# Seven block products in the pooled groups' output projection, and a chunk mask as eight score rows

## The reference, cut to what matters

```python
k_chunk = jnp.arange(s) // CHUNK                       # CHUNK = 64
sc = jnp.einsum('bqhd,bkhd->bhqk', qb, k) * scale
sc = jnp.where(k_chunk[None, :] <= q_chunk[:, None], sc, -jnp.inf)
```

```python
u, z = jnp.split(h @ w_in, 2, axis=-1)
p = causal_multiscale_pool(u).reshape(B, S, N_POOL_GROUPS, GROUP_WIDTH)
y = jnp.einsum('bsgc,gcd->bsgd', p, w_group).reshape(B, S, A_WIDTH_2) * scale
return (y * jax.nn.silu(z)) @ w_out                    # x = x + gate * this
```

## Time and profile before

| | |
|---|---|
| median of three runs | 2355.61 us (2354.32 to 2355.93) |
| span of the profiled execution | 2354.7 us, 0.9 us under that median |
| TensorE busy | 2328.3 us, 99% of the span, 11617 matmuls |
| TensorE weight loads | 1943.6 us (83%) |
| VectorE, GpSimd, ScalarE busy | 1535.8 us (65%), 1254.7 us (53%), 860.4 us (37%) |
| mean granted TensorE clock | 0.999 of full speed |

### The profile page before, as it was taken

One profiled execution on the slowest core, in us unless ns is written; L12 is line 12 of the kernel. 1 busy time (PEld: TensorE's weight loads), 2 busy tenths in 40 slices (PEclk: granted clock), 3 DMA queues, 4 the chain that ended last, 5 costly groups with the idle time before them and its releaser, 6 DMA issues.

```text
span 2354.7 us, 32347 instructions
## 1 busy us (share of the span) xinstructions
PE 2328.3 (99%) x11617; PEld 1943.6 (83%) x11617; DVE 1535.8 (65%) x1839; ACT 860.4 (37%) x1596; POOL 1254.7 (53%) x724
## 2 busy tenths in 40 slices
PE   9999999999999999999999999999999999999998
PEld 7888789888888888888888888778878788889887
DVE  7825556524578678788777777874572967147885
ACT  5212555612543222222222443122231244157773
POOL 4533955144145666766777434573654733467743
PEclk9999999999999999999999999999999999999999
DMA  5511011031011333333331111112121122210033
GB/s 220 157 45 46 19 19 37 1 116 45 19 42 50 117 124 117 125 125 117 123 124 64 63 45 45 58 53 78 54 76 67 58 67 109 79 37 24 24 115 137
DMA packets 67340, 178.85 MB, mean 76 GB/s; under 512 B 6994, under 2 KB 13908, under 8 KB 65120
## 3 DMA queue, kind: packets, MB, share of 16 engines
q1 hardware_dynamic: 57760, 147.80, 19.0%
q10 hardware_dynamic: 9104, 27.51, 3.4%
q0 software_dynamic: 368, 2.10, 0.5%
HBM read 161.61 MB, written 15.77 MB: 75 GB/s over the span
## 4 chain that ended last, share of the span: by engine, by line
PE 76%; DVE 6%; issue 4%; POOL 2%; ACT 1%; DMA 0%; POOLq 0%; DVEq 0%; ACTq 0%; SPq 0%
PE ps L704 21%; PE ps L705 20%; PE ps L707 20%; PE ps L854 4%; PE ps L832 3%; PE ps L842 2%; DVE trail L3532 1%; POOL split_lo L1653 1%; PE ps L2404 1%; PE ps L2420 1%; PE ps L2419 1%; PE ps L2389 1%; PE ps L2390 1%; ACT p L955 1%; PE ps L508 0%
## 5 line engine op out<-in xcount | busy, mean ns | idle before, releaser
L704 PE MATMUL ps<-h_hi,split_hi 128*128 128x512 f32 x1546 | 606.4, 392 | 3.7 <-DVE h_lo L3214 1.3
L705 PE MATMUL ps<-h_lo,split_hi 128*128 128x512 f32 x1546 | 601.1, 389 | 0.0
L707 PE MATMUL ps<-h_hi,split_lo 128*128 128x512 f32 x1546 | 536.2, 389 | 0.0
L1511 POOL TENSOR_TENSOR split_hi<-raw,cf 128x1024 fp32r<-128x1024 f32 x64 | 125.4, 1959 | 427.8 <-PE ps L707 373.4
L704 PEld LDWEIGHTS ps<-h_hi,split_hi 128*128 128x128 f32 x1546 | 290.7, 188 | 64.5 <-issue 2.5
L707 PEld LDWEIGHTS ps<-h_hi,split_lo 128*128 128x128 f32 x1546 | 290.8, 188 | 61.3
L705 PEld LDWEIGHTS ps<-h_lo,split_hi 128*128 128x128 f32 x1546 | 290.8, 188 | 56.4 <-issue 0.2
L1600 POOL TENSOR_TENSOR split_lo<-raw,split_hi 128x512 fp32r<-128x512 f32 x144 | 230.4, 1619 | 196.5 <-ACT split_hi L2717 196.3
L1653 POOL TENSOR_TENSOR split_lo<-raw,split_hi 128x512 fp32r<-128x512 f32 x84 | 128.1, 1534 | 179.5 <-ACT split_hi L2878 179.5
L2717 ACT CAST split_hi<-raw 128x512 fp32r<-128x512 f32 x144 | 87.0, 622 | 281.6 <-PE ps L707 205.4
L1513 POOL TENSOR_TENSOR split_lo<-raw,split_hi 128x1024 fp32r<-128x1024 f32 x64 | 178.4, 2787 | 5.0
(11 more groups left out here) (508 smaller groups left out, 5223.2 us busy)
## 6 DMA issues: line engine op xcount, KB each, us to landing
raw<-in_strips SPq DMA_DIRECT2D x208, 256.0 KB, 2.8
raw<-in_strips SPq DMA_DIRECT2D x86, 512.0 KB, 3.4
ada_raw<-in_ada SPq DMA_DIRECT2D x64, 512.0 KB, 3.6
memw_raw<-in_mem_strips SPq DMA_DIRECT2D x8, 512.0 KB, 5.8
xT<-in_xT ACTq DMA_DIRECT2D x4, 1024.0 KB, 7.9
x_spill_d<-xT ACTq DMA_DIRECT2D x1, 3584.0 KB, 10.1
xT<-x_spill_d ACTq DMA_DIRECT2D x2, 1792.0 KB, 9.3
out_T<-out_sb SPq DMA_DIRECT2D x13, 256.0 KB, 2.2
```

The source lines that it names most:

```text
L704: pe.matmul(acc[:, a:b], w_hi, hi[:, a:b], start=first, stop=False)
L705: pe.matmul(acc[:, a:b], w_hi, lo[:, a:b], start=False, stop=False)
L707: mm = pe.matmul(acc[:, a:b], w_lo, hi[:, a:b], start=False, stop=last)
L1511: pool.tensor_tensor(hi, raw[:, r, :], ones[:, 0:1].to_broadcast([P, D]), ALU.mult).then_inc(hi_split, 1)
```

## The change

It makes two edits.

1. The mask of the latent attention. Eight more rows are added to `mla_k` and `mla_q` (rows 96 to 103), loaded by two DMAs from a constant: in the query row t holds -1e30 for the early half of tile t, and in the key row t holds 1 for the late half of tile t. The score product runs over 104 rows, and its extra matmul with `cb` is gone.

2. The output projection of groups 1 to 3. The eight tiles of 24 matmuls become two quads of seven block products with 12 matmuls each (two output parts by two channel tiles by three). The token forms are made from the gates: the difference of the late and early tokens for channel tiles 0 and 1, and three more forms (`neg_two`, `neg_three`, `neg_four`), which take places in `h_hi` and `h_lo`. Those are saved to DRAM once (`h_keep_d`) and read back after each group by GpSimd's queue (`keep_again`). Products 0, 2, 4, 6 and products 1, 5 add up in the same banks, and VectorE adds each product to `xT` once (`out_sum`, 28 for each group). The hardware loops over g on TensorE and GpSimd are written out. Some semaphores are shared.

The core of the diff, with `...` where lines are left out:

```diff
+GROUP_SLOT = [p % 4 for p in range(42)] + [2, 3, 2, 3]
+OUT_BANKS = (((4, 6), (5, 7), (0, 1)), ((0, 2), (1, 3), (4, 5)))
+OUT_AFTER = {2: 0, 4: 2, 5: 1, 6: 4}
...
-                sc = [[(mla_q[0:96, h, q_tok], mla_k[0:96, h, lo:hi], lo, hi)] for lo, hi in key_banks(n)]
-                sc[-1].append((ident_bf, chunk_mask, t * P, n))
+                sc = [[(mla_q[0:MLA_ROWS, h, q_tok], mla_k[0:MLA_ROWS, h, lo:hi], lo, hi)] for lo, hi in key_banks(n)]
...
+            sp.wait_ge(feat_evac, 12)
+            for n, tensor in enumerate((mla_q, mla_k)):
+                sp.dma_start(tensor[NOPE + ROPE:MLA_ROWS, :, :],
+                             dram["chunk_rows"][n].unsqueeze(1).to_broadcast([QT, HEADS, T])).then_inc(mem_chunk_in, 16)
...
+        def gate_lower(eng, g, n):
+            eng.wait_ge(pool_ylo, 6 * g + (n - 2))
...
+            def load_out(g, quad):
+                for i, d in ((2, 0), (3, 1), (4, 2), (6, 3)):
+                    group_split(sp, g, out_form(quad, i))
+                    load_group_half(g, 12 + 2 * quad + d // 2, d % 2)
...
+            def out_forms(g, quad):
...
+                pool.tensor_tensor(pool_form, a21, a22, ALU.add).then_inc(form_sum, 1)
+                group_low(g, at + 1, OUT_SOURCE[1])
+                summed(g, 4 + quad, 1)
+                pool.tensor_tensor(a21, a21, a11, ALU.subtract).then_inc(form_sum, 1)
+                group_split(pool, g, at + 1)
+                pool.tensor_tensor(pool_form, a11, pool_form, ALU.subtract).then_inc(form_sum, 1)
+                group_low(g, at + 2, OUT_SOURCE[2])
...
+                pool.tensor_tensor(pool_form, a12, pool_form, ALU.add).then_inc(form_sum, 1)
+                for i in range(3, 7):
+                    group_low(g, at + i, OUT_SOURCE[i])
...
+            def out_quad(g, quad):
+                for i in range(7):
+                    p = out_form(quad, i)
+                    group_split(pe, g, p)
+                    if quad == 0:
+                        if i in (2, 4, 6):
+                            neg_lower(pe, g, i)
+                        else:
+                            gate_lower(pe, g, {0: 1, 1: 4, 3: 5, 5: 6}[i])
+                    for part in range(2):
...
+                        elif i in OUT_AFTER:
+                            out_read(pe, g, 14 * quad + 2 * OUT_AFTER[i] + part + 1)
+                        slot, w = group_at(p)
+                        product(pe, bank(OUT_BANKS[quad][OUT_BANK[i]][part]), slot,
+                                [(w + 2 * part + kk, *out_token(g, i, kk)) for kk in range(2)], HALF, start=i in (0, 1, 3), skip=True)\
+                            .then_inc(form_done if part else pool_tile, 1)
...
+            def out_tokens_made(g):
+                first_difference(g, 0)
+                first_difference(g, 1)
+                gates_low(g, 3, y_lo[:, 0:2, t1], gates[:, 0:2, t1], y_hi[:, 0:2, t1])
+                gate_step(g, 2).then_inc(pool_g, 1)
...
+                neg_two(g, 0)
+                neg_three(g, 0)
+                difference_low(g, 0)
+                neg_four(g, 0)
+                neg_low(g, 2, 0)
+                gate_step(g, 3, t2).then_inc(pool_g, 1)
+                gate_made(dve, g, 4)
+                neg_two(g, 1)
+                neg_three(g, 1)
+                difference_low(g, 1)
+                gate_step(g, 3, t1).then_inc(pool_g, 1)
+                gate_made(dve, g, 5)
+                neg_four(g, 1)
+                neg_low(g, 2, 1)
+                out_sum(g, 0, 0, 0)
+                out_sum(g, 0, 0, 1)
+                gates_low(g, 4, y_lo[:, 2, :], gated_tile(2), gated_hi_tile(2))
+                gates_low(g, 6, y_lo[:, 3, t1], gated_tile(3)[:, t1], gated_hi_tile(3)[:, t1])
+                out_sum(g, 0, 1, 0)
...
+            for g in range(1, POOL_GROUPS):
...
+                    if q == 0 and g > 1:
+                        group_through(pool, g - 1, out_form(1, 6))
+                        keep_again(g, 4, late_again)
...
+                if g < POOL_GROUPS - 1:
+                    group_through(pool, g, out_form(1, 4))
+                    keep_again(g, 2, h_again)
+                    keep_again(g, 3, h_again)
```

More of the change, by code:

```diff
@@ new lines, in first_difference, with gates_low, neg_two @@
+            def first_difference(g, t):
+                link(gate_step(g, t))
+                dve.tensor_tensor(gated_tile(t)[:, t2], gated_tile(t)[:, t2], gated_tile(t)[:, t1], ALU.subtract).then_inc(pool_g, 1)
+            def gates_low(g, n, out, src, hi):
+                gate_high(dve, g, n)
+                dve.tensor_tensor(out, src, rows(hi), ALU.subtract).then_inc(pool_ylo, 1)
+            def neg_two(g, kk):
+                dve.tensor_tensor(neg_full(g, 2, kk), gated_tile(kk)[:, t2], gated_tile(2 + kk)[:, t2], ALU.subtract).then_inc(neg_sum, 1)
@@ new lines, in difference_low, with out_sum @@
+            def difference_low(g, t):
+                gates_low(g, 1 + t, y_lo[:, t, t2], gated_tile(t)[:, t2], y_hi[:, t, t2])
+            def out_sum(g, quad, i, part):
+                p = out_form(quad, i)
+                if part:
+                    group_through(dve, g, p)
+                else:
+                    dve.wait_ge(pool_tile, 6 + 14 * (g - 1) + 7 * quad + i + 1)
+                if quad == 1 and i == 0 and part == 1:
+                    dve.wait_ge(x_again[0], 16 * g)
+                if i in (3, 4, 5):
+                    out_read(dve, g, 14 * quad + 2 * {3: 0, 4: 1, 5: 2}[i] + part + 1)
+                o, tok = 4 * quad + 2 * part + (i in OUT_SECOND), out_tokens[i in OUT_LATE]
+                dve.scalar_tensor_tensor(out=xT[:, o, tok], in0=bank(OUT_BANKS[quad][OUT_BANK[i]][part]), scalar=adav[:, 16 + o:17 + o],
+                                         in1=xT[:, o, tok], op0=ALU.mult, op1=ALU.add).then_inc(pool_res, 1)
@@ L3705, in _ @@
                 last_products(g, 3, gated_tile(2), gated_tile(3))
[L3706 to L3720 removed]
+                out_tokens_made(g)
+                for quad in range(2):
+                    for i in range(7) if quad else (5, 6):
+                        for part in range(2):
+                            out_sum(g, quad, i, part)
+                            if g == POOL_GROUPS - 1 and quad and i == 6 and part == 0:
+                                key_low(4)
+                        if g == POOL_GROUPS - 1 and quad and i < 4:
+                            key_low(i)
+            for k in range(5, NK):
+                key_low(k)
             norm_inverse(dve, n_kv)
@@ L3940, in _strips @@
         out += u[0:3] + z[0:1] + u[3:4] + z[1:4] + gg if g else z[0:2] + u + z[2:4] + gg
-        out += [_strip_tiles(a_out, [2 * o, 2 * o + 1], 4 * g, 4) for o in range(4)]
+        if g == 0:
+            out += [_strip_tiles(a_out, [2 * o, 2 * o + 1], 0, 4) for o in range(4)]
+        else:
+            out += [np.concatenate([_strip_tiles(a_out, [o, o + 2], k, 2)[:, :HALF] for k in (4 * g, 4 * g + 2)], 1) for o in (0, 1, 4, 5)]
     out += [_strip_tiles(v["w_kv_2"], [t], 0, 8) for t in range(2)]
```

270 lines of the change are left out of this document (191 added, 79 removed).

## The result

The changed kernel takes 2398.61 us (median of 4 runs, 2398.44 to 2399.26) against 2355.77 for the kernel before on the same chip: 42.8 us slower, ratio 1.0185 (95% interval 1.0172 to 1.0197). The prediction was 2367 with a range to 2378. The direction held, the size did not.

A forecast was written before the change was run, and what follows sets the result against it. TensorE, busy 99% of the span, was taken as the bound. Terms -16.3 - 3.5 + 21.6 + 4.8 + 4.6 + 0.4 = +11.6 us on the 2354.7 span gave 2366.3, plus 0.9 for the median: 2367, range 2346 to 2378.

The forecast's parts named there:

- 72 matmuls: Output projection of groups 1 to 3: 168 matmuls a group in place of 192, -16.3 us in three groups.
- mask: Latent attention scores: 32 mask matmuls go, -3.5 us, with bounds of 1.9 and 3.5.
- First place, product 1: Before product 1 of each group TensorE waits for VectorE's `pool_ylo` count 4: 7.2 us a group, +21.6 us in three.
- The added 2.5 us for collisions: Before product 1: VectorE's SBUF operations slowed beside GpSimd's, 2 to 3 us a group, taken as 2.5.
- Second place, the clock: Behind each group's wait before product 1 TensorE's clock falls to about half: 1.6 us a group, +4.8 us.
- Third place, the turns: Turns of groups 1 and 2: GpSimd's splits, sums and DMA issues make forms late, 2.3 us each, +4.6 us.
- "Costed at nothing", saved `h`: Saving 3 MB of `h` once on ScalarE's queue: 0 us, as the next strips are needed 10 us later.
- The key-value step: Key-value part: last `norm_add` 0.3 to 0.5 us late, as ScalarE has squares and copies queued: +0.4 us.
- A: Product 1's wait is VectorE's list alone, 4.7 us a group, clock stays: 2350 to 2355 us, chance 0.2.
- B: The wait before product 1 doesn't bind, only small waits stay: 2336 to 2343 us, chance 0.12.
- C: GpSimd becomes the bound in the output quads and the turns grow: 2375 us, chance 0.08.
- D: The mask edit does nothing, if VectorE or ScalarE sets that stage: 2370 us, no chance given.

The follow-up runs named there:

- the kernel with three edits: Changed kernel with product 1 waiting for count 3, reading back of h on SyncE's queue, and group 3's VectorE key steps one product later: 2372.14 us.
- the kernel with six edits: The kernel with three edits, plus saves of h taken apart, reading back behind the last strip half, and key steps 0 to 3 begun earlier: 2361.40 us.

## Why the prediction was wrong, step by step

Terms of its sum beside what the profile and the runs show:

| term | predicted | measured |
|---|---|---|
| 72 matmuls | -16.3 | -16.3 (72 x 0.2267) |
| mask | -3.5 | -2.8 (mask alone) |
| product 1, three waits | +21.6 | +21.0 |
| clock behind them | +4.8 | +6.6 (33 matmuls by 0.2) |
| two turns | +4.6 | +17.6 (13.0 of waits, 23 matmuls by 0.2) |
| saving `h` | 0 | +3.9 (2.1 of wait, 9 matmuls by 0.2) |
| key-value | +0.4 | +11.7 (5.3 + 2.0 + 0.4 of waits, 20 matmuls by 0.2) |

The measured column sums to 41.7, the medians differ by 42.8. Two things stand outside the table: the half clock at 1361 of the earlier trace rows (1.6 us) did not occur in the profiled run of the changed kernel, and the waits that are in no term are 4.0 us in place of 2.8. With these it is 41.3, and 1.5 us stay open.

**First place, product 1: right.** The place, the releaser, the three times and the size came as worked out, and the removal of the too strict count showed its part of the cause. The added 2.5 us for collisions came too. Two of VectorE's operations in group 1 that take 0.68 us alone, and the GpSimd one beside the second:

```profile
1614.60 1.60 DVE L3868 TENSOR_TENSOR h_plain<-h_plain 128x512 f32<-128x512 f32 x1
1621.49 1.77 DVE L3871 TENSOR_TENSOR h_plain<-h_plain,gates 128x512 f32<-128x512 f32 x1
1621.44 1.27 POOL L1718 TENSOR_TENSOR split_lo<-raw,split_hi 128x512 fp32r<-128x512 f32 x1 [5.79 <-ACT split_hi L3011]
```

The third is the difference of 1024 columns at 1625.10, 1.75 us in place of 1.22. Together 2.5 us over, and the same in groups 2 and 3; no run takes them away alone. What the prediction did not ask is what waits behind: with the count mended 2.8 to 3.1 us a group stay, which no version here removed.

**Second place, the clock: right in kind, 1.8 us too small.** Taken from one drop of 3.5 us behind 1.8 us of idling, the price was carried over to waits four times as long. The half clock around those lasted 6.8 to 10.2 us, of which 2.6 to 4.6 fell into the wait itself, where they cost nothing more, and 10 to 13 matmuls into the rest. The Trainium skill ("TensorE: Matmul & The Clock Gate", What's actually happening, the section behind the one that the prediction names) has the lower level as what an idle engine returns to; the six waits of over 5 us here agree, each at 0.50. The larger miss is that the prediction charged it at three places and it came at eight: two turns, two waits of the key steps and the 2.1 us of the saving had their own. The wait of 1.7 us at 1723 had none.

**Third place, the turns: the step that failed most.** "Four DMA issues of 0.55" was taken from the earlier trace rows, where three follow each other; at 295 us of the same trace four do, at 0.52 us each. The count is no limit by that. What differs is the amount: in both places of before they are 1.0 MB together (928, 48 and 48 KB; 24, 488, 24 and 488 KB), at the turns 2.0 MB. The fourth issue stood until the three transfers before it had landed. 2.3 us a turn were really 8.8. The bound of 3.5 was made from GpSimd's arithmetic alone, so it did not hold the unknown of the step. Taking the reading back off the queue gave back 6.9 us alone, and the turns were free only when it also went behind the last strip half.

**"Costed at nothing", saved `h`: failed.** The prediction named the cover ("a strip's 2.8 us would have to grow beyond that") and took it as safe. The strips' landing grew to 5.1 us in the median, and TensorE waited for a form made from one:

```profile
1539.74 0.51 PE L761 MATMUL ps<-pool_sums,split_hi 128*128 128x512 f32 x1 [2.09 <-POOL split_lo L1718]
```

Spreading the saves got 6.4 us back in the kernel with three edits, where a second wait of 1.8 had come up behind this one.

**The key-value step, 0.4 us: failed.** It looked only at ScalarE's load behind the last products. It missed that `out_sum` of product 4 is queued on VectorE behind `key_low(2)` and `key_low(3)`. The first waits for a square that ScalarE has behind a copy, and the copy waits for a slot that TensorE frees: a circle of three engines, 1.9 us. The second met GpSimd's difference of the key-value strip and took 2.1 us longer than alone. No run takes the two apart. Of the orders of the key steps tried here none left under 4.4 us of waits in this place (7.7 in the changed kernel), which speaks for too much work on VectorE there.

**Rivals.** A (wait of 4.7 and no clock loss) is refuted by the 7.0 us a wait (21.0 in three). B holds for no version: even with the count mended, 2.8 to 3.1 us a group stay. C, GpSimd as the bound, names the right engine at the wrong place: it was the queue, and at the turns. D is refuted by the kernel with the mask alone.

## What to carry to other kernels

Where the bounding engine is 99% busy, saved matmuls are worth only what the feeding engines can keep up with: price the work added to them (here 61 and 55 us for 16.3), and each wait twice, as idle time and as clock behind it. A step "costed at nothing" needs its cover's length in the row, and a DMA issue needs the amount that its queue was given just before, not only the price of a lone issue. When a wait is removed, read the list of waits anew before counting the gain.

## What the hardware showed unexpectedly

- GpSimd's queue took 1.5 MB in three transfers, or 1.75 MB in seven, within 2.3 and 3.8 us; the issue that would have made 2 MB stood 5.6 and 5.1 us (5.7 and 6.0 at the second turn), until 0.35 to 0.40 us after all the others had landed, and everything behind it on the engine with it. The six transfers issued on SyncE's queue, 3 MB within 3.8 us and before the first had landed, did not hold that engine up like this: 0.36 to 0.47 us each in the kernel with six edits. In the kernel with the reading back ahead of the strip half one of them took 1.9.
- A wait of 2 to 3 us may or may not cost the clock. In the kernel with the reading back on SyncE's queue the first turn's wait of 2.9 us left it at 1.00 (1673 to 1680), and behind the second turn's, 2.0 us, it stood at 0.50 (1825.4 to 1828.7). In each of the six waits of over 5 us in the changed kernel the clock fell to 0.50 while TensorE still waited, and it stayed there for 4.1 to 5.6 us of matmuls behind.
- The half clock at 1361 of the earlier trace rows comes and goes. It stands at this place, 3.4 us long, in seven of the thirteen profiled runs (the kernel before and six others, with and without the change) and in six not, the changed kernel's among them. Two runs can differ by its 1.6 us without any edit's doing.
- Two transfers of 1.5 MB on one queue raised the landing of 256 KB on another from 2.8 to 5.1 us in the median.
